# Early key rows and 80 sums in the PEER top-k of a hybrid decoder layer

## What is computed

```
s1, s2 = q[:, :, 0] @ keys[0].T, q[:, :, 1] @ keys[1].T   # 8 heads, 128 scores a side
v1, i1 = top_k(s1, 16);  v2, i2 = top_k(s2, 16)
cand   = v1[..., :, None] + v2[..., None, :]               # 256 sums for a head
top_s, top_i = top_k(cand, 16)
expert = (i1 * 128 + i2) at top_i;  gate = softmax(top_s)
act    = gelu(sum_d tok[d] * u_tab[expert, d])             # 8 x 16 key rows for a token
out    = sum_k gate * act * v_tab[expert]
```

## Time and profile before

| | us |
|---|---|
| median of 3 runs | 2377.42 (2374.26 to 2382.67) |
| the profiled execution's own time | 2373.41 |
| its span in the trace | 2371.6 |
| TensorE busy | 2115.3 (89%) |
| DVE busy | 1569.7 (66%) |
| ACT busy | 745.9 (31%) |
| POOL busy | 803.7 (34%) |

### The profile page before, as it was taken

The page is one execution under the profiler, slowest core; times in us unless marked ns, Lnnn a source line. Parts: engine busy times, 40 slices in busy tenths (PEclk is TensorE's granted clock), DMA queues, the critical chain, the costliest instruction groups (busy, mean ns, idle before and its releaser), DMA issues.

```text
span 2371.6 us, 34439 instructions
## 1 busy us (share of the span) xinstructions
PE 2115.3 (89%) x12253; PEld 1753.5 (74%) x12253; DVE 1569.7 (66%) x3260; ACT 745.9 (31%) x1111; POOL 803.7 (34%) x498
## 2 busy tenths in 40 slices
PE   7978998998678997999999989999888888898983
PEld 7978995555343347999999989999766666676762
DVE  1155215564443331169888979997888888898988
ACT  2122113443321002234444355554333232332321
POOL 2323320000110003346676621113544445565550
PEclk9999998999887998999999999999999999999996
DMA  9999987884996563225555578889999999999992
GB/s 351 348 357 347 350 326 292 328 353 180 324 323 230 176 240 99 71 95 171 173 171 171 170 243 293 295 287 366 388 394 394 394 394 380 395 395 394 392 393 76
DMA packets 200412, 682.81 MB, mean 288 GB/s; under 512 B 18432, under 2 KB 84352, under 8 KB 194304
## 3 DMA queue, kind: packets, MB, share of 16 engines
q1 hardware_dynamic: 151696, 508.36, 60.6%
q0 software_dynamic: 46080, 167.79, 18.5%
q10 hardware_dynamic: 2544, 5.48, 0.6%
HBM read 618.78 MB, written 196.32 MB: 344 GB/s over the span
## 4 chain that ended last, share of the span: by engine, by line
PE 35%; DMA 24%; issue 20%; DVE 14%; POOL 3%; ACT 3%; SPq 0%; ACTq 0%; DVEq 0%; POOLq 0%
DMA overlay<-peer_v 17%; PE bank L188 8%; PE bank L189 8%; PE bank L190 8%; DVE arena L1778 3%; DMA overlay<-peer_u 3%; DVE overlay L1955 3%; DMA overlay<-w_in 2%; PE bank L1765 2%; POOL overlay L341 2%; POOL overlay L1401 2%; DVE arena L1773 2%; PE bank L602 2%; PE bank L586 1%; PE bank L652 1%
## 5 line engine op out<-in xcount | busy, mean ns | idle before, releaser
L188 PE MATMUL bank<-overlay 128*128 128x384 f32 (+4 forms) x2856 | 989.0, 346 | 133.2 <-DVE overlay L1959 82.5
L189 PE MATMUL bank<-overlay 128*128 128x384 f32 (+4 forms) x2856 | 968.2, 339 | 0.0
L190 PE MATMUL bank<-overlay 128*128 128x384 f32 (+4 forms) x2856 | 966.4, 338 | 0.0
L188 PEld LDWEIGHTS bank<-overlay 128*128 128x128 f32 x2856 | 556.4, 195 | 199.3 <-issue 114.7
L190 PEld LDWEIGHTS bank<-overlay 128*128 128x128 f32 x2856 | 555.4, 194 | 33.5
L189 PEld LDWEIGHTS bank<-overlay 128*128 128x128 f32 x2856 | 556.9, 195 | 29.9
L1401 POOL TENSOR_TENSOR overlay<-overlay 128x1024 fp32r<-128x1024 f32 x98 | 262.6, 2682 | 207.2 <-ACT overlay L1393 207.1
L1610 POOL DMA_INDIRECT arena<-peer_rows,arena x160 | 182.6, 1141 | 366.3 <-DVE arena L1773 340.5
L1610 POOL DMA_INDIRECT arena<-peer_v,arena x160 | 228.7, 1429 | 172.0 <-DVE arena L1778 159.3
L1778 DVE SCALAR_TENSOR_TENSOR arena<-arena 128x1024 f32<-128x1024 f32 x160 | 203.9, 1275 | 0.4
L1773 DVE SCALAR_TENSOR_TENSOR arena<-arena 128x1024 f32<-128x1024 f32 x160 | 193.3, 1215 | 6.1 <-DMA arena<-peer_rows,arena 6.1
(11 more groups left out here) (221 smaller groups left out, 2028.8 us busy)
## 6 DMA issues: line engine op xcount, KB each, us to landing
overlay<-peer_u SPq DMA_DIRECT2D x128, 512.0 KB
overlay<-peer_v SPq DMA_DIRECT2D x128, 512.0 KB
o_ks<-cache_k SPq DMA_DIRECT2D x16, 4088.0 KB, 27.8
o_vsall<-cache_vall SPq DMA_DIRECT2D x16, 4088.0 KB, 40.1
arena<-cache_kT SPq DMA_DIRECT2D x32, 896.0 KB, 11.3
arena<-cache_v SPq DMA_DIRECT2D x56, 512.0 KB, 6.6
arena<-w_out SPq DMA_DIRECT2D x48, 512.0 KB, 4.8
act<-arena SPq DMA_DIRECT2D x128, 192.0 KB
```

The costliest lines, as they stand in the source:

```text
L188: pe.matmul(out, lhs[0], rhs[0], start=start, stop=False)
L189: pe.matmul(out, lhs[0], rhs[1], start=False, stop=False)
L190: return pe.matmul(out, lhs[1], rhs[0], start=False, stop=stop)
```

## The change

Two things are done together.

1. 24 of the 128 key rows of tile 3 are gathered and multiplied in the top-k stage. In `pool_query`, POOL's loop over units ends at unit 31; then POOL waits for the top-k of both sparse tiles, and runs units 32 to 79 with a gather behind every second `lo`, through a ring of four buffers (where the scores of tiles 3 and 4 were). In `dve_topk` a dot product (`early_dot`) stands behind every 14th of the 120 searches of a dense tile, eight for a tile. It reads the token tile from PSUM banks 4 and 5, to which ACT copies it once. The later gathers are 296 and not 320, and the values stage has 236 rows and not 260.
2. Of the 256 sums of a head 80 are formed (16 of the first row, 7 x 8 of the next rows, 8 of the first column) and searched, by three additions in place of one; the place found is turned back into row and column by six more small operations.

The core of the diff:

```diff
 
-            with pool.Fori(0, (QF + EARLY) // 4) as x:
+            with pool.Fori(0, (QF + 2 * AHEAD) // 4) as x:
                 for s in range(4):
                     lo(x * 4 + s, s)
+            pool.wait_ge(topk.sem, after["sparse"])
+            for n in range(DT * AHEAD):
+                lo(QF + 2 * AHEAD + n, n % 4)
+                if n % 2 == 0:
+                    g = n // 2
+                    if g >= 4:
+                        pool.wait_ge(erow_done, g - 3)
+                    pool.indirect_dma_start(ering[g % 4], None, t["peer_rows"], bass.IndirectOffsetOnAxis(ap=rows3[:, g:g + 1], axis=0))\
+                        .then_inc(erow_in[g % 4], 16)
             for s in range(LEAD):
                 lo(QF + EARLY + s, s)
...
-        cand = cut(111, PH, TOPK, TOPK)
+        FULL = TOPK // 2
+        CAND = TOPK + (FULL - 1) * FULL + TOPK - FULL
+        cand = cut(111, PH, CAND)
...
+        PER_ROWS, APART = TOPK // 2, 14
+        EARLY_ROWS = DT * PER_ROWS
+        ering = [cut(34 + 4 * r, D) for r in range(4)]
+        erow_in, erow_done, h_copied = [sem(f"erow_in{s}") for s in range(4)], sem("erow_done"), sem("h_copied")
...
-        PER_TILE = 1 + 5 * QF + 2 + 5 * PH + 5 + 2 * 3 + 3
+        PER_TILE = 1 + 5 * QF + 4 + 5 * PH + 11 + 2 * 3 + 3
...
+            searched = [0]
+
+            def between(row):
+                searched[0] += 1
+                if row and searched[0] % APART == 0 and searched[0] // APART <= PER_ROWS:
+                    row(searched[0] // APART - 1)
...
-            def top16(values, width, out_v, out_i, n):
+            def top16(values, width, out_v, out_i, n, row=None):
                 for k in range(2):
                     fence()
                     for f in range(n):
                         step(dve.max(out_v(f, k), values(f)))
+                        between(row)
                     fence()
...
+                top16(lambda f: sc[:, f], PK, lambda f, k: sv[:, f, K8 * k:K8 * k + K8], lambda f, k: su[:, f, K8 * k:K8 * k + K8], QF, row)
                 step.wait(dve)
                 step(dve.tensor_copy(si, su))
                 v = sv.rearrange("p (h s) k -> p h s k", s=2)
-                step(dve.tensor_tensor(cand, v[:, :, 0].unsqueeze(3).to_broadcast([P, PH, TOPK, TOPK]),
-                                       v[:, :, 1].unsqueeze(2).to_broadcast([P, PH, TOPK, TOPK]), ALU.add))
+                spread = lambda x, n: x.unsqueeze(3).to_broadcast([P, PH, x.shape[2], n])
+                step(dve.tensor_tensor(cand[:, :, 0:TOPK], v[:, :, 0, 0:1].to_broadcast([P, PH, TOPK]), v[:, :, 1], ALU.add))
+                step(dve.tensor_tensor(cand[:, :, TOPK:CAND - FULL].rearrange("p h (a b) -> p h a b", b=FULL), spread(v[:, :, 0, 1:FULL], FULL),
+                                       v[:, :, 1, 0:FULL].unsqueeze(2).to_broadcast([P, PH, FULL - 1, FULL]), ALU.add))
+                step(dve.tensor_tensor(cand[:, :, CAND - FULL:], v[:, :, 0, FULL:], v[:, :, 1, 0:1].to_broadcast([P, PH, FULL]), ALU.add))
                 step.wait(dve)
-                flat = cand.rearrange("p h a b -> p h (a b)")
-                top16(lambda f: flat[:, f], TOPK * TOPK, lambda f, k: cv[:, f, K8 * k:K8 * k + K8],
-                      lambda f, k: cu[:, f, K8 * k:K8 * k + K8], PH)
+                top16(lambda f: cand[:, f], CAND, lambda f, k: cv[:, f, K8 * k:K8 * k + K8],
+                      lambda f, k: cu[:, f, K8 * k:K8 * k + K8], PH, row)
                 step.wait(dve)
 
-                step(dve.tensor_scalar(ca, cu, 4, None, ALU.logical_shift_right))
-                step(dve.tensor_scalar(cb_, cu, 15, None, ALU.bitwise_and))
+                step(dve.tensor_scalar(ca, cu, 3, None, ALU.logical_shift_right))
+                step(dve.tensor_scalar(cb_, cu, 7, None, ALU.bitwise_and))
                 step.wait(dve)
                 step(dve.tensor_copy(caf[:, 0], ca))
                 step(dve.tensor_copy(caf[:, 1], cb_))
+                step.wait(dve)
+                step(dve.scalar_tensor_tensor(last_, caf[:, 0], float(FULL + 1), caf[:, 1], ALU.is_equal, ALU.mult))
+                step(dve.tensor_scalar(first_, caf[:, 0], 1.0, float(FULL), ALU.is_equal, ALU.mult))
+                step(dve.tensor_scalar(row_, caf[:, 0], -1.0, 0.0, ALU.add, ALU.max))
+                step.wait(dve)
+                step(dve.tensor_tensor(caf[:, 0], row_, last_, ALU.add))
+                step(dve.tensor_tensor(first_, first_, last_, ALU.subtract))
+                step.wait(dve)
+                step(dve.tensor_tensor(caf[:, 1], caf[:, 1], first_, ALU.add))
...
+            dve.wait_ge(h_copied, 1)
             with dve.Fori(0, DT) as i:
                 step.enter(i, PER_TILE)
-                after["shifted"] = step.outer + tile(sall[:, bass.ds(i, 1)].rearrange("p o f n -> p (o f) n"), i + 3, i + 1)
+
+                def early_dot(r):
+                    at = ering[r % 4].rearrange("p (b n) -> p b n", b=2)
+                    dve.wait_ge(erow_in[r % 4], i * (16 * PER_ROWS // 4) + 16 * (r // 4 + 1))
+                    dve.scalar_tensor_tensor(at, at, 1.0, bank[:, 4:6, :], ALU.mult, ALU.mult, accum_out=w3[:, bass.ds(i * PER_ROWS + r, 1)]).then_inc(erow_done, 1)
+
+                after["shifted"] = step.outer + tile(sall[:, bass.ds(i, 1)].rearrange("p o f n -> p (o f) n"), i + 3, i + 1, early_dot)
...
+            pool.wait_ge(erow_done, EARLY_ROWS)
             tables = (t["peer_rows"], t["peer_v"].rearrange("a p n -> (a p) n"))
 
             def gather(g):
-                table, j = tables[g // UROWS], g % UROWS
+                table, j = tables[(g + EARLY_ROWS) // UROWS], (g + EARLY_ROWS) % UROWS
                 at = rows3[:, j:j + 1] if j < SLOTS else rowsS[:, j - SLOTS:j - SLOTS + 1]
                 if g >= RING:
                     pool.wait_ge(row_done, g - RING + 1)
                 pool.indirect_dma_start(gring[g % RING], None, table, bass.IndirectOffsetOnAxis(ap=at, axis=0)).then_inc(row_in[g % RING], 16)
 
-            for g in range(2 * UROWS):
+            for g in range(2 * UROWS - EARLY_ROWS):
...
+            act.wait_ge(s_kept, 2 * QF + 4)
+            act.copy(bank[:, 4:6, :], h1[:, DT].rearrange("p (b n) -> p b n", b=2)).then_inc(h_copied, 1)
...
-                        dot(dve, g % RING, g // RING, h1[:, DT], w3, g)
+                        dot(dve, g % RING, g // RING, h1[:, DT], w3, g + EARLY_ROWS)
...
-        LATE_ROWS = 2 * UROWS - DONE
+        LATE_ROWS = 2 * UROWS - EARLY_ROWS - DONE
...
-            act.wait_ge(row_done, SLOTS)
+            act.wait_ge(row_done, SLOTS - EARLY_ROWS)
...
-                g = j = DONE + r
+                g = DONE + r
+                j = g + EARLY_ROWS
...
```

## The result

The changed kernel takes 2390.3 us at the median (2387.4 to 2392.5) against 2377.6 us of the kernel before: a ratio of 1.0054, with a 95% interval of 1.0039 to 1.0069. It is slower by 12.7 us, where 12.6 were forecast. A second measurement of both kernels, on another chip, gave 1.0072 (1.0047 to 1.0096), 2392.5 against 2374.6 us, where 1.005 was expected. The profiled execution took 2390.16 us with a span of 2388.4.

A forecast was written before the change was run, and what follows sets the result against it. TensorE was taken to bound the dense blocks, the DMA engines the values stage. Dense blocks paying 44.6 us less 32.0 gained gave +12.6 on the 2377.4 us median: 2390.0 us, range 2374 to 2405.

The forecast's parts named there:

- The gain of the values stage: 24 gathers fewer in the values stage, 1.33 us each: 32.0 us less, bounds 26 and 33.
- The 80 sums are worth nothing: DVE's second top-16: 7.4 us less for each of five tiles, which only lengthens DVE's wait for the exponential.
- POOL's place: Dense blocks: POOL issues each gather behind its unit's `lo`, so the eighth begins 51.2 us into the block.
- Landing: From an early gather's begin to DVE's first use: 4.4 us, plus 0.5 for a unit's fetch and store beside it.
- The tail behind the dot product: DVE after a tile's eighth dot product: remaining searches and a fence 1.8 us, then decoding 1.1 + 1.3 us.
- The hot section: DVE's stretch between the decoding and the softmax of the gates in a dense tile: 18.5 us, bounds 18.1 and 22.
- The clock: TensorE at half clock until about 4.4 us behind a restart: 2.2 us lost twice, bounds 0 and 3 each.
- The stage's sum: What the dense blocks pay: 42.0 of TensorE waits - 1.8 + 4.4 = 44.6 us, bounds 36 and 58.
- Rows in time: Rival: gathers land before DVE's searches reach them, so only the values stage's 32 us gain remains: 2345 us; chance 0.11.
- Late descriptors: Rival: POOL and DVE hold each other up ahead of the eighth row, 15 us more: 2405 us; chance 0.05.
- The draw: Rival: same mechanism with the cheap end of its terms, +3 us: 2380 us, taking in -7 to +7; chance 0.15.
- the values stage that does not shrink: Rival: another wait holds the values stage at its length, so the 44.6 us stand alone: 2422 us; chance 0.03.

The follow-up runs named there:

- eight_unrolled: first_eight with DVE's loop over the three dense tiles written out: 2345.4 us, 0.9854 of the kernel before; 2344.8 us in a second measurement.
- rows_left_out: The changed kernel with the 24 early rows neither gathered nor multiplied, their weights set to 0: 2347.6 us, 0.9866 of the kernel before.
- sums_only: The changed kernel without early rows, the 80 sums kept and 320 late gathers as before the change: 2375.1 us, 0.9985 of the kernel before.
- rows_only: The changed kernel with early rows kept, but all 256 sums formed and searched and the old decoding: 2396.1 us, 1.0073 of the kernel before.
- first_eight: The changed kernel with a tile's eight gathers behind units 0 to 7 of its block, not every second unit: 2352.3 us, 0.9904 of the kernel before.
- tokens_in_sbuf: first_eight with the early dot products reading the token tile from SBUF in place of PSUM: 2363.0 us, 0.9948 of the kernel before.

## Why the prediction was right, point by point

- **What bounds the stages: right.** TensorE bounds the dense blocks unless DVE is late, as eight_unrolled and rows_left_out show. The values stage shrinks by the rows' price. That its bound is DMA is read from the profile (a share of 1.04, with DVE busy 536 of 600 us) and not shown apart: every run that takes the 24 gathers out of the stage takes DVE's 31 us for them out too.
- **The gain of the values stage: right.** 32.0 forecast, 33.6 in the traces (34.5 with the rows left out). The stage's length itself varies: in the ten traces with 236 late rows it is 608.3 to 613.7 us.
- **The 80 sums are worth nothing: right**, by sums_only and rows_only. The searches' size was right too: an index search of 80 values follows the last after 0.21 us. The small operations' was not where POOL was in the way: the three additions, 1.0 us forecast, take 0.9 in the sparse tiles of the changed kernel and 3.2 to 3.7 in the dense ones.
- **POOL's place: right.** The eighth gather of the first block began 1217.66 - 1166.93 = 50.7 us into it; 51.2 was forecast. In the next two it was 54.4 and 54.7 behind the block's begin, with 53.4 forecast for the half clock.
- **Landing: undersized.** 4.9 was taken, from one gather's begin to DVE's use it was 6.6, 5.6 and 5.1 us.
- **The tail behind the dot product: undersized.** 1.8 + 2.4 us forecast; from the eighth dot product's end to the hot section 8.6, 6.5 and 6.5 us passed. In the first block the small operations collide with POOL: the old shift took 1.77 in place of 0.23 us beside a `lo`, and the new selection 3.02 in place of 0.29 (it began while POOL wrote a gather's descriptors, and ended with the `lo` behind them). In the other two blocks other small operations are held up in the same way.
- **The hot section: oversized.** 18.5 was taken; 16.1, 16.1 and 14.0 were measured from its first operation to the softmax. I had taken the multiplication's length of before for its own; it is 2.29 us when no `lo` is running as it begins, which in the changed kernel is the case in four of six. The operation at 1270.67 that I called an addition is the comparison ahead of the multiplication, and the `lo` of 3.47 us that I put beside it stands beside the next comparison and multiplication, 12 us later.
- **The clock: right for the two pauses that were counted.** Round the restart of the first block:

```profile
1250.00:1252.00 2.00, 0.87 (x4) 0.80 (x5) 0.80 (x4) 0.00 (x0) 0.00 (x0) 0.50 0.00 0
1252.00:1254.00 2.00, 2.00 (x8) 2.00 (x7) 0.00 (x0) 0.48 (x1) 0.00 (x0) 0.50 0.04 8
1254.00:1256.00 2.00, 2.00 (x9) 2.00 (x9) 0.84 (x1) 0.00 (x0) 0.00 (x0) 0.64 0.01 4
1256.00:1258.00 2.00, 2.00 (x13) 2.00 (x12) 1.86 (x10) 0.00 (x0) 0.00 (x0) 1.00 0.00 0
```

TensorE restarts at 1251.13 at 1.2 GHz and is back at 2.4 GHz at about 1255.4 (0.64 over two us), 4.3 us later; 2.1 us are lost, 2.2 forecast. The same happens behind the second pause. Behind the third, for which I had counted nothing, TensorE runs at 0.50 until about 1426.0, 6.3 us after its restart:

```profile
1421.27 0.69 PE L188 MATMUL bank<-overlay 128*128 128x384 f32 x1 [0.67 <-ACT arena L1740]
```

The wait for ACT's copy did shrink from 2.35 us to 0.67, as forecast, but the 1.8 us did not come back: from the third transposes to the values stage it is 0.3 us more, not less.

- **The stage's sum:** 44.6 us forecast, 50.1 + 0.3 in the traces, within the bounds of 36 and 58. TensorE's waits are 45.6 us for 42.0. In the first block the two undersized terms (1.7 and 4.4 us) and the oversized one (2.4) partly cancel. The bounds do not follow from those of the terms, which give about 37.5 at the low end and over 60 at the high one. That the medians moved by 12.7 us, almost the 12.6 forecast, is luck: the two traces differ by 16.8 us and the medians of the second measurement by 17.9. In the executions here the stages ahead of the top-k alone differ by some 9 us (unit 31 ends at 1167 us in one, near 1176 in another).
- **The rivals.** Rows in time was a rival by its mechanism and its price: first_eight puts the gathers where it asked, and 2345 is what eight_unrolled takes. Late descriptors did not come in the changed kernel: 23 of its 24 early gathers took POOL 0.95 us, the first 1.92. The draw and the values stage that does not shrink are out by the ratio and by the 33.6 us. The page of the Trainium skill beside the gather's latency ("DMA: Bandwidth & Descriptors", "Anatomy of one DMA — SWDGE (gpsimd) path") would have given an estimate of 3.2 us; the runs had 5.1 to 6.6 beside other traffic, so here the measurement decides.
- **POOL and DVE hold each other up** more widely than I had in mind. What the Trainium skill states in "SBUF — State Buffer", section "Who interferes with whom", that a DVE instruction with two SBUF inputs contends with a GpSimd instruction that reads SBUF, agrees with L1579 (2.29 and 4.31 us in one tile) and with tokens_in_sbuf. In the first block the multiplication that begins at 1236.39, ahead of a `lo`, takes 2.29 us and that `lo` 3.71 in place of 2.40; the one at 1243.39, with a `lo` running until 1245.55, takes 4.31.

## What to carry to other kernels

An operation that is slipped in between the steps of a paced queue arrives at that queue's pace: before moving work beside an idle engine, ask at which moment the slowest of its inputs is issued, not only whether the engines have room. Eight gathers a tile issued behind the first eight units cost the stage nothing (with DVE's loop written out), the same gathers issued behind every second unit cost it 50 us. Shortening the work of an engine that then waits for another buys only a longer wait, and once one wait at a block's end is gone it pays to look for the next.

## What the hardware showed that I had not expected

- The multiplication of the hot section (two inputs in SBUF) took 4.37 to 4.54 us all ten times before the change, twice for each of five tiles (least, median, longest ns):

```profile
L1542 DVE TENSOR_TENSOR arena<-arena x10: 4366/4374/4544, 1077.3 to 1352.0; 128x2048 f32<-128x2048 f32 x10
```

  So it looked like its own length. Each time a `lo` of POOL had begun ahead of it and was still running; in the changed kernel, where none was, it is 2.29. A duration that is constant in a trace may still be contention.
- DVE's return to the head of its loop cost 4.2 us of idle time with nothing waited for in the changed kernel, and 6.2 and 4.9 in first_eight, where the kernel before had 0.58. It went when the loop was written out. In rows_only, sums_only and rows_left_out, whose loops hold fewer instructions, it is 0.6 as before. What DVE does in that time no run shows.
- An early gather's descriptors took POOL 0.95 us as a rule, and 2.8 to 3.1 us in some places of the experiments beside the hot section's comparison or multiplication, as here in first_eight, where the multiplication began at 1225.87 and ended at 1230.25:

```profile
1228.25 2.83 POOL L1412 DMA_INDIRECT arena<-peer_rows,arena  x1
```
